# A two-layer hybrid-attention step on one core: layer 0's loads in another order, with its own order of steps

## The reference, cut to what matters

```python
for l in range(2):
    h = rms_norm(x, ln_attn[l])
    z = h @ w_in[l]                       # 1024 -> 1184: q_a 512, k_a 128, v_a 128, cq 256, ckv 128, k_rope 32
    q_a, k_a = rope(rms_norm(q_a)), rope(rms_norm(k_a))        # group A: 8 heads on 2 key heads, window 128
    q_b = rms_norm(cq) @ b_w_uq;  k_b, v_b = split(rms_norm(ckv) @ b_w_ukv)   # group B: latent attention
    o = concat(sink_attend(q_a, k_a, v_a), attend(q_b, k_b, v_b))
    x = x + o @ w_o[l]
    h = rms_norm(x, ln_ffn[l])
    x = x + (swiglu(h) if l == 0 else top2_of_8_experts(h))    # inner width 2816
```

## Time and profile before

| | |
|---|---|
| median of three runs | 1398.15 us |
| the profiled execution | 1402.91 us |
| its span | 1401.1 us |
| granted TensorE clock, mean | 0.955 of full |
| PE / DVE / ACT / POOL busy | 1288.4 / 941.8 / 808.0 / 145.3 us |
| moved by DMA | 357 MB, 255 GB/s over the span |
| layer 0's attention phase, to the first L1743 | 0 to 204.2 us |

### The profile page before, as it was taken

The page is one execution under the profiler, slowest core; times in us unless marked ns, Lnnn a source line. Parts: engine busy times, 40 slices in busy tenths (PEclk is TensorE's granted clock), DMA queues, the critical chain, the costliest instruction groups (busy, mean ns, idle before and its releaser), DMA issues.

```text
span 1401.1 us, 18545 instructions
## 1 busy us (share of the span) xinstructions
PE 1288.4 (92%) x6917; PEld 1055.7 (75%) x6917; DVE 941.8 (67%) x913; ACT 808.0 (58%) x797; POOL 145.3 (10%) x138
## 2 busy tenths in 40 slices
PE   0978989999998889859999999999999999999993
PEld 0536849999995467548888888888888888888882
DVE  1473444444424735338889888898898888988983
ACT  1244643434313437327776787777877867878773
POOL 3010000000000000200021030020120210401201
PEclk9997999999999969959999999999999999999997
DMA  8040046544240410359999999999999999999995
GB/s 296 1 160 31 1 129 210 172 160 156 106 161 16 153 39 1 127 211 352 351 358 406 361 381 387 363 390 367 368 409 359 377 389 362 394 365 371 403 357 188
DMA packets 125710, 356.98 MB, mean 255 GB/s; under 512 B 8721, under 2 KB 34033, under 8 KB 125633
## 3 DMA queue, kind: packets, MB, share of 16 engines
q1 hardware_dynamic: 121120, 342.34, 65.8%
q0 software_dynamic: 4480, 14.00, 3.4%
q10 hardware_dynamic: 64, 0.02, 0.0%
HBM read 348.04 MB, written 9.48 MB: 255 GB/s over the span
## 4 chain that ended last, share of the span: by engine, by line
PE 82%; issue 6%; DVE 4%; ACT 2%; DMA 2%; SPq 2%; POOL 0%; DVEq 0%; ACTq 0%; POOLq 0%
PE ps L1828 30%; PE ps L1848 15%; PE ps L1743 10%; PE ps L1557 8%; PE ps L1759 5%; PE ps L1720 2%; PE ps L1714 2%; PE ps L1620 1%; PE ps L1667 1%; PE ps L1836 1%; SPq L629 1%; PE ps L1497 1%; PE ps L1612 1%; PE ps L1682 1%; DMA ring<-in_moe_w_gate 1%
## 5 line engine op out<-in xcount | busy, mean ns | idle before, releaser
L1089 DVE TENSOR_TENSOR w_lo<-ring,w_hi 128x2048 fp32r<-128x2048 f32 (+1 forms) x326 | 684.3, 2126 | 187.2 <-ACT w_hi L788 184.7
L788 ACT ACTIVATE w_hi<-ring 128x2048 fp32r<-128x2048 f32 (+1 forms) x326 | 574.6, 1783 | 229.3 <-PE ps L1848 69.2
L1828 PE MATMUL ps<-w_hi,xg_hi 128*128 128x512 f32 (+1 forms) x768 | 288.7, 376 | 2.5 <-DVE xg_lo L1437 2.5
L1828 PE MATMUL ps<-w_hi,xg_lo 128*128 128x512 f32 (+1 forms) x768 | 286.6, 373 | 0.0
L1828 PE MATMUL ps<-w_lo,xg_hi 128*128 128x512 f32 (+1 forms) x768 | 286.1, 372 | 0.0
L1828 PEld LDWEIGHTS ps<-w_hi,xg_hi 128*128 128x128 f32 x768 | 145.0, 189 | 28.3 <-issue 2.9
L1828 PEld LDWEIGHTS ps<-w_lo,xg_hi 128*128 128x128 f32 x768 | 144.6, 188 | 25.9
L1828 PEld LDWEIGHTS ps<-w_hi,xg_lo 128*128 128x128 f32 x768 | 145.0, 189 | 25.1
L1848 PE MATMUL ps<-w_hi,am_hi 128*128 128x512 f32 x352 | 138.6, 394 | 0.0
L1848 PE MATMUL ps<-w_lo,am_hi 128*128 128x512 f32 x352 | 137.3, 390 | 0.0
L1848 PE MATMUL ps<-w_hi,am_lo 128*128 128x512 f32 x352 | 137.2, 390 | 0.0
(11 more groups left out here) (275 smaller groups left out, 1435.5 us busy)
## 6 DMA issues: line engine op xcount, KB each, us to landing
ring<-in_moe_w_down SPq DMA_DIRECT2D x80, 1024.0 KB, 7.7
ring<-in_moe_w_gate SPq DMA_DIRECT2D x68, 1024.0 KB, 7.4
ring<-in_moe_w_up SPq DMA_DIRECT2D x66, 1024.0 KB, 9.5
ring<-in_moe_w_gate SPq DMA_DIRECT2D x32, 768.0 KB, 7.7
ring<-in_moe_w_up SPq DMA_DIRECT2D x32, 768.0 KB, 5.8
ring<-in_ffn_w_gate SPq DMA_DIRECT2D x11, 1024.0 KB, 5.2
ring<-in_ffn_w_up SPq DMA_DIRECT2D x11, 1024.0 KB, 5.5
ring<-in_ffn_w_down SPq DMA_DIRECT2D x10, 1024.0 KB, 5.0
```

Of the source, the lines that this page charges most:

```text
L788: A(hi[:, 0:size], src[:, 0:size], ACT.Copy).then_inc(hi_ready, 1)
L1089: V.tensor_tensor(lo[:, 0:size], src[:, 0:size], hi[:, 0:size].bitcast(F32), ALU.subtract).then_inc(lo_ready, 1)
L1828: ins = mm_(ps[:, b + c0 // 512, 0:c1 - c0], (xg_hi, xg_lo)[xp][:, k, :], w[wp][:, k % 2, c0:c1], start=(k == 0 and n == 0), stop=(k == KD ...
```

## The change

Only layer 0's attention phase changes in what is issued, and in what order:

1. The constants are split. The identity and `eps` (129 columns) are loaded first; the other 1437 columns (`loaded_tables`, a new semaphore) after all of `w_in`. POOL waits for the second part before the rotary tables, DVE before its first `z1`, `i1` or `sm`.
2. SP's order is: identity, `x` of tile 0, two pieces of `w_in`, `x` of tiles 2 and 1, three pieces of `w_in`, the other constants, `b_w_ukv`, `b_w_uq` (the two have changed places), layer 1's norm vectors.
3. Layer 0's norm vectors are issued by ACT, after its two layer-norm loads; ACT then runs one `Sqrt` on a dummy, which brings its table load to the start.
4. The three order tables become lists of two; layer 1 keeps the old order, layer 0 has its own. `nth` and `no` count per layer.
5. Buffers of the attention phase start at multiples of 16 words, not 8.

```diff
         @block.sync
         def _(sp):
-            for t in TILES:
+            def load_x(t):
                 src = a["x_sample"][0] if t == 2 else a["x_prompt"][0, t * P:(t + 1) * P, :]
                 sp.dma_start(xres[0:ROWS[t], t, :], src).then_inc(loaded_x[t], 16)
-            sp.dma_start(cst[:, :], consts).then_inc(loaded_c, 16)
+
+            sp.dma_start(cst[:, 0:FIRST_W], consts[:, 0:FIRST_W]).then_inc(loaded_c, 16)
+            load_x(0)
...
-                if key == ("uq", 0):
-                    load_gains(0)
+                if key == ("in", 0, 1, 0):
+                    load_x(2)
+                    load_x(1)
+                elif key == ("uq", 0):
+                    sp.dma_start(cst[:, FIRST_W:CONST_W], consts[:, FIRST_W:CONST_W]).then_inc(loaded_tables, 16)
                 elif key == ("wo", 0, 0, 0):
-                    load_gains(1)
+                    load_gains(sp, 1)
                 if key in before:
                     slot_room(before[key])
-                src, n, w = source(key)
-                sp.dma_start(slot(key, n, w), src).then_inc(w_ready[slot_of[key]], 16)
                 if key[0] == "uq":
                     if key[1]:
                         wait_full(sp, ("tz", KD - 1))
                     sp.dma_start(w_ukv, a["b_w_ukv"][key[1]]).then_inc(ukv_ready, 16)
+                src, n, w = source(key)
+                sp.dma_start(slot(key, n, w), src).then_inc(w_ready[slot_of[key]], 16)
...
-            pool.wait_ge(loaded_c, 16)
+            pool.wait_ge(loaded_tables, 16)
...
+            load_gains(act, 0)
             act.wait_ge(warm_set, 1)
+            A(warm[:, 1:2], warm[:, 0:1], ACT.Sqrt)
...
             for l in range(DEPTH):
-                for step in DVE_ORDER:
+                for step in DVE_ORDER[l]:
                     kind, *which = step
+                    if kind in ("z1", "i1", "sm"):
+                        tables_in()
...
-                start, self.at = self.at, self.at + (n + 7) // 8 * 8
+                start, self.at = self.at, self.at + (n + 15) // 16 * 16
...
-PE_ORDER = [("tc",), ("h", 0), ("item", 0), ("h", 2), ("za", 0, 1, 0), ("za", 2), ("za", 0, 1, 1), ("za", 0, 0, 0), ("zc", 0),
+PE_ORDER = [[("h", 0), ("za", 0, 0, 0), ("h", 2), ("tc",), ("za", 0, 0, 1), ("za", 0, 1, 0), ("za", 2), ("item", 0),
```

More of the change, by code:

```diff
@@ L77 @@
 CONST_W = _at
+FIRST_W = P + 1
 GAIN = {}
@@ L220, in build @@
     assert len(EXPERT) % RING == 0
[L221 to L222 removed]
+    SMALL = [(s_[0], l, *s_[1:]) for l in range(DEPTH) for s_ in PE_ORDER[l] if in_small(s_)]
+    BANKED = [[(s_[0], l, s_[1], c) for l in range(DEPTH) for s_ in PE_ORDER[l] if s_[0] in IN_BANK and s_[2:] == (c, 0)]
               for c in range(2)]
@@ L231, in build @@
     MAXES, NORMED = nth(DVE_ORDER, "sm"), nth(DVE_ORDER, "dn")
-    EXPS = nth([s_ for s_ in ACT_ORDER if s_[0] == "e" and GROUPS[s_[1]][1] < 2], "e")
+    EXPS = nth([[s_ for s_ in order if s_[0] == "e" and GROUPS[s_[1]][1] < 2] for order in ACT_ORDER], "e")
     with ExitStack() as ctx:
@@ L502, in no @@
         def no(counts, l, step):
-            return len(counts) * l + counts[step]
+            return sum(len(c) for c in counts[:l]) + counts[l][step]
         def wait_tile(eng, l, t):
@@ L830, in _ @@
             for l in range(DEPTH):
-                for step in ACT_ORDER:
+                for step in ACT_ORDER[l]:
                     kind, *which = step
@@ L1509, in _ @@
             for l in range(DEPTH):
-                for step in PE_ORDER:
+                for step in PE_ORDER[l]:
                     kind, *which = step
```

44 lines of the change are left out of this document (25 added, 19 removed), and 55 rows, old and new, of tables (ACT_ORDER, DVE_ORDER, PE_ORDER).

## The result

| | before | changed |
|---|---|---|
| median | 1398.13 us (4 runs, 1397.13 to 1398.73) | **1377.58 us** (4 runs, 1377.04 to 1378.32) |
| ratio | | 0.9842, 95% interval 0.9823 to 0.9861 |
| profiled execution / its span | 1402.91 / 1401.1 us | 1377.23 / 1375.4 us |
| mean granted clock of it | 0.955 | 0.958 |
| first feed-forward matmul | 204.22 us | 176.65 us |

The kernel is 1.6% faster. The time is 4.3 us above the forecast of 1373.3 and inside the range of 1364 to 1385. The sum's own forecast for a profiled execution was 1378.1, and that came out at 1377.23. So most of the miss is not in the walk through the steps; it is in the step from the profile to the median, and the first experiment shows how.

A forecast was written before the change was run, and what follows sets the result against it. PE's chain of waits was taken to bound the kernel, so time before layer 0's feed-forward counts. Gains 21.2 + 8.0 + 3.6 less 8 make 24.8: profiled execution 1378.1, median 1398.15 to 1373.3 us, range 1364 to 1385.

The forecast's parts named there:

- Front: Layer 0's start up to the end of item 0: PE gets there at 36.8 instead of 58.0, gain 21.2 us.
- The first rival: Front loads become the bound, queues taking turns: PE loses 4 to 8 us, time 1377 to 1381; chance 0.11.
- What the loads give: Front: by the skill page, moving the norm vectors alone is worth only 2 us; the order gives the rest of 21.2.
- Middle and tail: End of item 0 to end of item 5, then to the feed-forward: gains 8.0 and 3.6 us, before the clock's loss.
- that milestone: End of item 0 and the work both orders have ahead of the first L1570: 58.0 before, 36.8 forecast.
- The 2.6 at tq of tile 1: Middle: PE waits 2.6 us there, with z2 of tile 1 and od of group 0 ahead on DVE.
- the 1.4 added: Middle: 1.4 us added because o of tile 2 was allowed 3.5 us for each group.
- The clock: Low clock after new waits in layer 0: 4 us for the first group, 2 each for two others, loss 8.
- a refutation: The middle is wrong if PEclk is at 0.5 for more than 16 us between 40 and 130.
- the second rival: Clock falls for as long as before: two bouts cost 20 instead of 8, time 1385, half way 1379; chance 0.15.
- The step that failed: Profile to median: the 4.8 us excess of the profiled execution scales with no term, so 1378.1 becomes median 1373.3.
- The addresses: Buffers at multiples of 16 words and per-layer counts: same instructions at other addresses, taken as 0, bounded by +-1.

The follow-up runs named there:

- the first experiment: The kernel before, unedited, run and profiled again: 1400.32 us over ten runs, ratio 1.0006.
- experiment 9: Changed kernel with the nine norm-vector loads issued by ACT behind tile 0's root instead of ahead of its first activation: 1376.45 us, ratio 0.9835.
- 11: The kernel of experiment 9 with POOL's 1 MB of zero stores moved behind its rotary tables: 1374.01 us, ratio 0.9821.
- experiment 7: Changed kernel with four dummy products in PE's 3.2 us wait at tq of tile 2: 1377.29 us, ratio 0.9838.
- experiment 8: Changed kernel with dummy products in two PE waits, one before the scores of group 2, two before those of group 5: 1378.22 us, ratio 0.9845.
- the lower group: Runs of the unedited kernel before at mean granted clock 0.958: 1397.8 to 1398.6 us; the other five ran 1402.1 to 1402.8 at 0.955.

## Why the prediction came out as it did

**Front.** Forecast 58.0 to 36.8; measured 57.95 to 36.9. Right to 0.1 us, which is luck: errors inside cancel. ACT was free at 7.76, not 6.0: nine of its issues took 0.48 to 1.07 us each and not 0.48. So hT of tile 0 came at 15.0, not 13.1. Against it, the half block took 5.96, not 6.9, the turned rows of tile 2 0.68, not 1.0, and the two half blocks after them 7.03, not 7.4. The chain of the changed kernel, as the profile follows it back, shows what really led:

```profile
2.71 16.30 DMA xres<-in_x_sample
19.04 1.16 ACT xn L850 x2
```

`x` of tile 2, 128 KB, took 16.3 us to land (11.8 without the norm vectors in front, experiment 9). That transfer was not in the sum at all. The pieces of `w_in` landed at about 18 and 23.6, the large part of the constants at 29.9, `b_w_ukv` at 31.1, where I had 17.2, 20.8, 27.4 and 28.8: 1 to 3 us late everywhere, which the room covered. The first rival's mechanism is there in its small form, and experiments 9 and 11 show that it is what a next version meets.

**What the loads give.** The Trainium skill ("Trainium Kernel Development and Optimization", Key Constraints) has it that another issuing engine shares the same 16 DMA engines, so that the rest had to come from the order. The runs agree in the main: the order alone gives 18, the loads on top of it 2.6; alone, under the old order, they bring 3.9 in the front, more than the 2 us in which the engines were dry. The rest would fit the 768 KB of `b_w_uq` that no longer go ahead of `b_w_ukv`; no run separates the two.

**Middle and tail.** From that milestone to the feed-forward I had a gain of 8.0 + 3.6 - 8 = 3.6; it was 146.3 less 139.7, 6.6. The waits came in order and place: 3.2 for 3.4, 0.8 for 2.0, 2.4 for 2.7. The 2.6 at tq of tile 1 did not come (that step ran at 93.7 without a wait), 1.0 at the scores of group 2 did, unforeseen. `o` of groups 0 and 1 took 4.2 and 3.7, for my 3.5 and the 1.4 added. Part of the 3.0 is a step that I left out: the low clock of before lasted past 123.7, where my middle ends, and the scores there (L1667 at 123.62) took 2.08 us, 1.16 in the changed kernel.

**The clock.** I charged 8, in three bouts behind the three waits. There were four bouts and some 20 us at 1.2 GHz, more than the 16 that I had named as a refutation, and the reading of it that I gave there was wrong: half of 20 is a loss of 10 only where PE is the bound. Of the first bout, 6.7 us long, the half up to 50 costs nothing (experiment 7). The other three, 13.5 us with PE busy nearly throughout, make 6.7 by the same halving, and item 1 can add up to 1.6. That estimate of 6.7 to 8.3 is near my 8, by another distribution; no run removes all of it. The largest costly bout, at 88, follows no wait that matters (experiment 8). The page behind the second rival ("TensorE: Matmul & The Clock Gate", A second HAM failure mode, in the Trainium skill) has a clock that swings after frequent short idles. The swing is there, in four bouts; the idles are not what the runs show ahead of the one at 88, where filling the wait changed nothing. Nor did 104 to 124 of the earlier trace rows agree with it, as the prediction had it: that is a steady 0.50 behind two waits of 2.4 and 5.3. As a forecast of 20 us lost the rival would have been far too high.

**The step that failed** is the last one, "its own time would be 1378.1, and the median goes from 1398.15 to 1373.3". It took the 4.8 us between the profiled execution and the median for something apart. 4.25 of them were in the terms: 2.2 up to the milestone, with the 5.76 us half block of the earlier trace rows, 2.0 in the half clock of 104 to 124, and both go with the change, whichever group the run before is in. With those rows from a profile of the lower group the gain would have been 24.8 less 4.25, 20.5, and the median 1377.6, as measured. The hint was on the page: 1402.91 against three runs within 0.6 us of 1398.15.

**The addresses** I took at 0 and bounded by 1: they cost 1.9, outside that bound. This error and the 3.0 too little for middle and tail have opposite signs, which leaves the profiled total within 0.9 us of the forecast.

## What to carry to other kernels

Before a sum is made from one profile, hold its time against the timed runs; where it lies apart, find which rows hold the excess, because a change that removes those rows gains nothing of it in the other runs. In an in-order queue ask of each blocked step what stands behind it that could run: one step moved gave 13.5 us here, all the earlier loads 2.6. And a low clock costs nothing where the engine follows another, as from 47 to 50 here, so price each bout by who waits for whom in it, and once a wait is gone, look which transfer or address-dependent stage is next.
